# Moving the first network's working area by 32 bytes within a 128-byte line

## The reference, cut to what matters

```python
for l in range(2):
    u = rms_norm(x, g_mix[l]) * (1 + sc_a) + sh_a
    proj = u @ w_in[l]                       # queries, keys, values, gates of three attentions
    ...
    x = x + gt_a * (merged @ w_out[l])
    u = rms_norm(x, g_ffn[l]) * (1 + sc_f) + sh_f
    h = silu(u @ w_ffn_gate[l]) * (u @ w_ffn_up[l])
    x = x + gt_f * (h @ w_ffn_down[l])
```

## Time and profile before

| | |
|---|---|
| Median of three runs | 2098.29 us (2096.26 to 2100.85) |
| Profiled execution, its own time | 2101.66 us |
| Its span, first to last instruction | 2099.9 us |
| TensorE busy | 2025.5 us, 96% of the span |
| VectorE / ScalarE busy | 77% / 56% |
| Mean granted TensorE clock | 0.992 |

### The profile page before, as it was taken

How to read it: one execution, slowest core, us unless ns; L and a number is a source line. 1 busy time by engine, 2 the same in 40 slices (tenths; PEclk the granted TensorE clock), 3 DMA queues, 4 the chain that set the end, 5 groups by cost and what they waited for, 6 DMA issues and landing times.

```text
span 2099.9 us, 37052 instructions
## 1 busy us (share of the span) xinstructions
PE 2025.5 (96%) x13975; PEld 1837.7 (88%) x13975; DVE 1624.7 (77%) x2668; ACT 1171.1 (56%) x2116; POOL 148.3 (7%) x233
## 2 busy tenths in 40 slices
PE   6999989999999989999999999999999999999998
PEld 6988989999988989998876888888888888899997
DVE  7788879966688879979787789786989426658983
ACT  6757746645557756646636555352544227646762
POOL 0100000000000000004000300001102000000000
PEclk9999999999999999999999999999999999999999
DMA  9766547865766547876341334546634222244553
GB/s 367 272 216 203 189 146 258 282 229 167 241 216 210 180 153 258 300 243 219 126 162 62 107 131 156 194 141 240 211 130 142 99 90 101 81 161 141 184 178 110
DMA packets 106624, 383.03 MB, mean 182 GB/s; under 512 B 11504, under 2 KB 16128, under 8 KB 105184
## 3 DMA queue, kind: packets, MB, share of 16 engines
q1 hardware_dynamic: 77584, 280.21, 39.2%
q0 software_dynamic: 25792, 94.31, 13.4%
q10 hardware_dynamic: 3088, 6.29, 0.8%
HBM read 379.71 MB, written 1.05 MB: 181 GB/s over the span
## 4 chain that ended last, share of the span: by engine, by line
PE 77%; DVE 12%; ACT 4%; issue 4%; DMA 3%; POOL 0%; POOLq 0%; SPq 0%; DVEq 0%; ACTq 0%
PE ps L1099 19%; PE ps L1102 18%; PE ps L1103 18%; DVE ring_l L2379 3%; PE ps L1120 3%; PE ps L1124 3%; PE ps L1125 3%; DVE ada_junk L2402 2%; DMA work<-adas_in 2%; PE ps L1142 2%; ACT ring_r L1722 2%; PE ps L1145 1%; PE ps L1146 1%; PE ps L1672 1%; DMA ring<-tape_in 1%
## 5 line engine op out<-in xcount | busy, mean ns | idle before, releaser
L1099 PE MATMUL ps<-part,ring_l 128*128 128x256 f32 (+1 forms) x3445 | 1038.6, 301 | 13.7 <-DVE ring_l L2379 7.3
L1103 PE MATMUL ps<-part,ring_r 128*128 128x256 f32 (+1 forms) x3445 | 1027.2, 298 | 0.0
L1102 PE MATMUL ps<-part,ring_r 128*128 128x256 f32 (+1 forms) x3445 | 1026.1, 298 | 0.0
L2379 DVE TENSOR_TENSOR ring_l<-ring,ring_r 128x1024 fp32r<-128x1024 f32 x514 | 626.4, 1232 | 149.5 <-ACT ring_r L1722 146.8
L1722 ACT ACTIVATE ring_r<-ring 128x1024 fp32r<-128x1024 f32 x514 | 533.8, 1056 | 356.8 <-DMA ring<-tape_in 259.1
L1099 PEld LDWEIGHTS ps<-part,ring_l 128*128 128x128 f32 x3445 | 652.0, 189 | 44.2 <-DVE part L2379 7.7
L1103 PEld LDWEIGHTS ps<-part,ring_r 128*128 128x128 f32 x3445 | 648.6, 188 | 24.7
L1102 PEld LDWEIGHTS ps<-part,ring_r 128*128 128x128 f32 x3445 | 648.5, 188 | 24.3
L2402 DVE SCALAR_TENSOR_TENSOR ada_junk<-work 128x1024 bf16<-128x1024 f32 x272 | 334.0, 1228 | 50.2 <-DMA work<-adas_in 38.2
L1142 PE MATMUL ps<-part,ring_l 128*128 128x256 f32 (+1 forms) x400 | 125.5, 314 | 20.9 <-DVE part L2379 11.1
L1146 PE MATMUL ps<-part,ring_r 128*128 128x256 f32 (+1 forms) x400 | 121.5, 304 | 0.0
(11 more groups left out here) (287 smaller groups left out, 2109.0 us busy)
## 6 DMA issues: line engine op xcount, KB each, us to landing
ring<-tape_in SPq DMA_DIRECT2D x514, 512.0 KB, 3.4
work<-adas_in POOLq DMA_DIRECT2D x176, 512.0 KB, 4.7
work<-ada_first_in SPq DMA_DIRECT2D x8, 1024.0 KB, 17.5
work<-bias_in ACTq DMA_DIRECT2D x1, 2048.0 KB, 7.9
x<-x_t_in SPq DMA_DIRECT2D x1, 1024.0 KB, 7.5
work<-cond_in POOLq DMA_DIRECT2D x1, 1024.0 KB, 8.9
x<-ctx_in ACTq DMA_DIRECT2D x1, 1024.0 KB, 13.1
x<-dist_in ACTq DMA_DIRECT2D x1, 1024.0 KB, 6.2
```

What stands on the lines that cost most here:

```text
L1099: mm = pe.matmul(dst, lhsT=wl, rhs=mr, start=(k == 0), stop=False)
L1102: pe.matmul(dst, lhsT=wr, rhs=mr, start=False, stop=False)
L1103: mm = pe.matmul(dst, lhsT=wr, rhs=ml, start=False, stop=(k == len(moving) - 1))
L2379: return dve.tensor_tensor(dst, whole, rounded_part.bitcast(F32), ALU.subtract)
```

## The change

The first layout's counter starts at 16 floats instead of 24. All tensors of the first network in `work` move down by 32 bytes, and begin (96 + 4·16) mod 128 = 32 bytes past a 128-byte line. The second network's layout, the ring, x and the constants stay where they are. The instructions of every engine, their order and their waits are the same in both kernels; addresses alone differ.

```diff
         xt = x[:, :, 0:T]
         sq = x[:, :, T:T2]
-        FROM_LINE = 24
+        FROM_LINE = 16
         taken[0] = FROM_LINE
         U = place(2, KD, T)
         u_r, u_l = pair(U, KD, T)
```

## The result

The changed kernel takes 2106.86 us, median of six runs (2105.03 to 2111.3); the kernel before, on the same chip, 2097.28 us. The ratio is 1.0044, with an interval of 1.0025 to 1.0064: **slower by 0.44%**, 9.6 us. The prediction was 2108 us, slower, range 2085 to 2128.

The account below looks back on a forecast made before the run. The prediction took TensorE to bound the kernel. Terms of 4.7 (gate and up), 4.9 (other tiles) and 0.5 us (streams) gave +10 us, and the same step on the median of 2098.29 us gave 2108 us, range 2085 to 2128.

Parts of the forecast that it names:

- the likeliest case: Whole kernel slower by about one to two steps per weight tile, 2103 to 2122 us; chance 38%.
- Gate and up: First network's gate and up projections, 704 weight tiles in both layers, all on the chain: 4.7 us more.
- one step of 6.7 ns: Smallest spacing between observed paces, taken as the added cost of each first-network weight tile of linear.
- The other 1,120 tiles: Input projections, gates, branches and output projection: 7.5 us more, of which 65% counts, 4.9 us.
- The bound of 13.3: Best end per weight tile of linear: every slow tile turns fast, from 353.3 to 340.0, gaining 13.3 ns.
- Streams: 72 groups of stream, stationary parts moved, at most one step of 6.7 ns each: 0.5 us.
- the terms at nothing: Attention's float32 matmuls, ACT and DVE operations, and DMAs into the moved buffers: each put at zero.
- the stretch at 62 us: Full-clock weight tiles from 62.37 to 77.67 us, at 340.0 ns each; claimed to become 346.7 or above.
- the stretch of 124 us: Gate and up projections of the first network, 310 to 434 us; claimed to become about 2.4 us longer.
- Faster: Rival: the shift puts every first-network stretch on the fast pace, −15 us, 2083 us; chance 23%.
- Nothing: Rival: operands come in pieces of 32 bytes or less, so paces stay, 2098 us; chance 27%.
- Dearer: Rival: each matmul pays a whole piece, 7.1 ns, 21.2 per tile, 32 us with streams, 2130 us; chance 12%.

Follow-up runs that it names:

- e5: Changed kernel plus a 32-byte spacer ahead of the ring, so activations and weights all lie 32 bytes further than in the kernel before; 1.0007 of before.
- e1: Kernel before with the first network's tensors begun at 0 past a 128-byte line instead of 64; 1.0064 of before.
- e6: Kernel before plus a 32-byte spacer ahead of the ring, with the first network's pairs back at 64, so the weights moved; 1.0043 of before.
- e4: Separate kernel without the network: 16-tile matmul runs at 16 pairs of starts, other engines idle, then busy; 340.0 to 360.0 ns per tile.
- e8: Separate kernel without the network: 512 combinations of operand places in 32-byte steps, each begun two ways, then 4-byte steps; none of the 512 below 340.0 ns per tile.
- e9: Kernel before with the 384-byte tensor mod moved between the two rings, setting them 128 bytes apart, pairs left at 64; 0.9981 of before.
- e7: Separate kernel without the network: moving start shifted 4 bytes at a time against weights on a line; 346.7 to 368.9 ns per tile.
- e11: Kernel before with the rings 128 bytes apart and the first network's pairs at 192 instead of 64; 0.9938 of before, 2087.95 us.
- e2: Kernel before with the first network's tensors begun 96 bytes past a 128-byte line instead of 64; 1.0087 of before.

## Why the prediction was right, and where it wasn't

*The size.* Forecast +10 us, 2108; measured +9.6, 2106.86. The range of the likeliest case alone, 2103 to 2122, holds it, too. It came out right by luck, as the next two points show.

*Gate and up, +4.7 us: wrong, sign and all.* This was the step "704 tiles of one more step each, and nothing covers it". These tiles went from 353.3 to 352.0, −0.9 us, and the stretch did 1056 matmuls where it had done 1054. The mistake is in the step before it: I took one step of 6.7 ns as due by every tile. In fact the levels themselves were replaced, 340.0 and 353.3 by 352.0 and 356.0, and what a tile pays depends on which level it had and which it got. Gate and up, the one place where the loss would have been fully on the chain, already had the slow one.

*The other 1,120 tiles, +7.5 or, with 35% covered, +4.9: too small.* They lost about 7.3 + 0.9 = 8.2 us, nearly all of it from tiles that had stood at 340.0: compared tile by tile, 537 of these lost 13.6 ns each on average, and those at 353.3 lost 0.6. The bound of 13.3 that I put on the side of the gain would have been about right for them, on the side of the loss. So one term was too large by 5.6 us and the other too small by 0.7 to 3.3, and the two errors offset each other in part. How much of the loss waits on panels covered is not shown: the chain's shares in attention moved in e5 as well, without a loss.

*Streams (+0.5) and the terms at nothing:* right. The 64 groups of `stream` with parts of U went from a mean of 693.7 to 701.5 ns, 0.5 us in all. Attention's float32 matmuls with both operands now at 32 (L1337, 256 columns) take 118.9 ns from start to start before and after. DVE takes 1231 ns for 1232, and the 512-column tiles of the second network stand at 29.53 us for 43 tiles, 686.7 ns, before and after, by these rows of the kernel after:

```profile
1345.03 0.39 PE L1099 MATMUL ps<-part,ring_l 128*128 128x512 f32 x1
...
1374.56 0.39 PE L1099 MATMUL ps<-part,ring_l 128*128 128x512 f32 x1
```

*What would show it.* I wrote: gate and up at 360 ns or above (it was 352.0, wrong), the stretch at 62 us at 346.7 or above (352.0, right), the stretch of 124 us 2.4 us longer (not so), the second network of the same length (the lag behind before is 3.9 us at 1000 us and 4.0 at 1540, right).

*The mechanism: wrong.* I took a start at 32 to cost more because a read then touches 17 pieces of 64 bytes instead of 16. But e1 has whole pieces and is slower, and e5 has none and isn't. What the runs showed in its place is the distance between the moving tile and the weights: e6 makes the whole loss with the first network's activations where they were.

*The rivals.* "Faster" came nearest to the mechanism, how weight loads and moving reads fall against each other, with the wrong sign: the shift went to a distance without a fast pace instead of one with nothing else. Another edit has that outcome, 192 with the rings apart (0.9938, where the rival's 2083 us would be 0.993). "Nothing" with pieces of 32 bytes or less is out. The 16-byte lines of "SBUF — State Buffer" (Specifications (TRN2)) in the Trainium skill don't tell the two kernels apart: their starts are both at whole lines, and they differ by 0.44%. "Dearer", 21.2 ns on every tile, is not reached by any start tried; the worst, 96 past a line, has 359.9, 10.0 above before on U and 16.1 on LAT and Y.

*What stays open.* Why a run of matmuls begins on one of its levels is not settled. In e4 each run had the same level in both halves, so its beginning decides it, but in e8 one and the same matmul right ahead led to different levels. In the network the "others" column changes (94, 473, 522 fast tiles) between kernels that have the same distance there. There is one profile per kernel, so whether each execution chooses alike isn't known; the runs of before on one chip spread from 2088.4 to 2103.66 us, which clock and waits could make as well. Why U at 64 didn't keep the fast pace in e9 is open. Nor do the traces show what in the chip makes the distance count; that it is the weight load that runs beside a matmul is argued from e6, not seen.

## What to carry to other kernels

Read a pace from start to start before pricing an edit to it, and ask which tiles are on which level: an edit that replaces the levels takes most from those that are fast. When TensorE streams one buffer while it loads weights from another, lay the two out against each other, and test that by moving either one alone; a change to any tensor that lies ahead of them shifts it. The fast layout here was found by scanning places in a small kernel, but the scan had to be tried in the real one, since one of its two best places failed there.

## What the runs showed of the hardware

- The pace of a 256-column float32r matmul at full clock depends on the distance between the start of the moving tile and that of the weights: 340.0 to 360.0 ns per three on the grid of 32 bytes with both parts together, up to 373.5 over the 512 combinations. The pattern came back after 256 bytes, not after 128 (e7). Over the layouts tried, this kernel's time went from 0.9938 (e11) to 1.0087 (e2) of before, with the same instructions.
- The same distance can have two or three steady paces (340.0 and 353.3 at 192; 352.0, 356.0 and 360.0 at 160), chosen by how the run begins, and in e4 not changed by busy DVE and ACT.
- For 512 columns two rings 128 bytes apart were dearer (695.5 against 686.7 ns), where 256 columns gained: a layout is good for one shape, not for all.
